# Banded attention in a fused transformer block: the projections of the last two query tiles, and the squares of those tiles, one step later

## The reference

```python
def swa_layer(x, norm_g, w_in, q_g, k_g, sinks, w_out):
    proj = rms_norm_2(x, norm_g) @ w_in
    q, k, v = jnp.split(proj, [C_Q_HEADS * C_HEAD_DIM, C_Q_HEADS * C_HEAD_DIM + kv_w], axis=-1)
    q = rms_norm_2(q.reshape(B, S, C_KV_HEADS, C_GROUP, C_HEAD_DIM), q_g)
    k = rms_norm_2(k.reshape(B, S, C_KV_HEADS, C_HEAD_DIM), k_g)
    ...
# for each block of 128 queries, against its own and the previous block of keys:
        s = jnp.einsum('bqhgd,bkhd->bhgqk', qi.astype(jnp.float32), kb) * scale + bias
        m = jnp.maximum(jnp.max(s, axis=-1, keepdims=True), sink)
        p = jnp.exp(s - m)
        denom = jnp.sum(p, axis=-1, keepdims=True) + jnp.exp(sink - m)
        return jnp.einsum('bhgqk,bkhd->bqhgd', p / denom, vb)
```

## Time and profile before

| | us |
|---|---|
| median of 3 runs | 2206.51 |
| lowest, highest | 2206.43, 2208.19 |
| the profiled execution | 2210.78 |
| its span, first to last instruction | 2209.0 |
| TensorE busy in the span | 2179.2 |
| ScalarE, VectorE, GpSimd busy | 839.3, 899.8, 942.8 |

### The profile page before, as it was taken

The page is one execution under the profiler, slowest core; times in us unless marked ns, Lnnn a source line. Parts: engine busy times, 40 slices in busy tenths (PEclk is TensorE's granted clock), DMA queues, the critical chain, the costliest instruction groups (busy, mean ns, idle before and its releaser), DMA issues.

```text
span 2209.0 us, 28941 instructions
## 1 busy us (share of the span) xinstructions
PE 2179.2 (99%) x10374; PEld 1791.5 (81%) x10374; DVE 899.8 (41%) x1270; ACT 839.3 (38%) x1235; POOL 942.8 (43%) x457
## 2 busy tenths in 40 slices
PE   8999999999999999999999899999999999999999
PEld 6888887788887888888887678888888878888887
DVE  5222222555625522222226854555322556555400
ACT  5222222323533422323334634444323665444421
POOL 3444444333472444445442244444444435444443
PEclk9999999999999999999999999999999999999999
DMA  5333333222352233323341032333333103333332
GB/s 174 100 95 98 101 105 112 77 77 68 105 163 67 75 106 95 95 95 105 105 136 50 29 96 86 96 102 97 105 105 134 49 20 105 95 95 98 101 115 77
DMA packets 58685, 210.25 MB, mean 95 GB/s; under 512 B 6640, under 2 KB 7408, under 8 KB 58224
## 3 DMA queue, kind: packets, MB, share of 16 engines
q1 hardware_dynamic: 56736, 202.07, 29.9%
q10 hardware_dynamic: 1872, 7.10, 0.9%
HBM read 207.05 MB, written 2.10 MB: 95 GB/s over the span
## 4 chain that ended last, share of the span: by engine, by line
PE 95%; DVE 3%; ACT 1%; issue 0%; DMA 0%; ACTq 0%; DVEq 0%
PE psum L217 29%; PE psum L219 29%; PE psum L218 29%; PE psum L241 1%; PE psum L242 1%; PE psum L243 1%; PE psum L1254 1%; PE psum L1279 1%; PE psum L2147 0%; PE psum L2161 0%; ACT swa_p L2244 0%; DVE ab_s L1889 0%; PE psum L2174 0%; DVE ab_negated L1896 0%; PE psum L822 0%
## 5 line engine op out<-in xcount | busy, mean ns | idle before, releaser
L182 POOL TENSOR_TENSOR w_lo<-w_raw,w_hi 128x1024 fp32r<-128x1024 f32 x375 | 902.6, 2414 | 1158.7 <-ACT w_hi L171 1158.6
L217 PE MATMUL psum<-x_hi,w_hi 128*128 128x512 f32 x1816 | 715.1, 394 | 9.6 <-DVE w_lo L189 9.6
L219 PE MATMUL psum<-x_hi,w_lo 128*128 128x512 f32 x1816 | 709.2, 391 | 0.0
L218 PE MATMUL psum<-x_lo,w_hi 128*128 128x512 f32 x1816 | 709.0, 390 | 0.0
L171 ACT ACTIVATE w_hi<-w_raw 128x1024 fp32r<-128x1024 f32 x379 | 394.4, 1054 | 531.3 <-PE psum L219 497.6
L217 PEld LDWEIGHTS psum<-x_hi,w_hi 128*128 128x128 f32 x1816 | 341.9, 188 | 86.6 <-DVE w_lo L189 9.6
L219 PEld LDWEIGHTS psum<-x_hi,w_lo 128*128 128x128 f32 x1816 | 341.5, 188 | 73.1
L218 PEld LDWEIGHTS psum<-x_lo,w_hi 128*128 128x128 f32 x1816 | 341.9, 188 | 71.0 <-issue 0.5
L263 DVE SCALAR_TENSOR_TENSOR x<-psum,x 128x512 f32<-128x512 f32 x64 | 44.3, 692 | 367.4 <-PE psum L219 366.8
L217 PE MATMUL psum<-ffn_hidden_hi,w_hi 128*128 128x512 f32 x352 | 136.9, 389 | 0.0
L218 PE MATMUL psum<-ffn_hidden_lo,w_hi 128*128 128x512 f32 x352 | 136.9, 389 | 0.0
(11 more groups left out here) (311 smaller groups left out, 2515.5 us busy)
## 6 DMA issues: line engine op xcount, KB each, us to landing
w_raw<-in_stream SPq DMA_DIRECT2D x379, 512.0 KB, 3.6
swa_bias<-in_swa_bias ACTq DMA_DIRECT2D x1, 2048.0 KB, 9.8
out<-x SPq DMA_DIRECT2D x8, 256.0 KB, 4.5
ab_bias<-in_ab_bias ACTq DMA_DIRECT2D x1, 1792.0 KB, 7.9
x<-in_x_in SPq DMA_DIRECT2D x4, 256.0 KB, 7.1
x<-in_x_in ACTq DMA_DIRECT2D x4, 256.0 KB, 7.3
xattn_mem<-in_mem ACTq DMA_DIRECT2D x1, 1024.0 KB, 4.9
mix_k_turned<-in_gate_w ACTq DMA_DIRECT2D x1, 256.0 KB, 3.6
```

What stands on the lines that cost most here:

```text
L182: pool.tensor_tensor(self.w_lo[:, split, :], self.w_raw[:, raw, :], self.w_hi[:, split, :].bitcast(F32), ALU.subtract).then_inc(self.w_lo_ ...
L217: pe.matmul(out, w_hi, hi[:, k0 + j, :], start=first and j == order[0], stop=False)
L218: pe.matmul(out, w_hi, lo[:, k0 + j, :], start=False, stop=False)
L219: mm = pe.matmul(out, w_lo, hi[:, k0 + j, :], start=False, stop=last and j == order[-1])
```

## The change

Two tables of numbers change. The projection of q6 moves from step 5 to step 6 and that of q7 from step 7 to step 8; their squares move from steps 6 and 8 to steps 7 and 9. The order of PSUM turns, the copies of weight units (`ahead`) and the `lower` on GpSimd follow from the same tables. No instruction is added or removed.

```diff
-    PROJECTED = {1: [4], 3: [5], 5: [6], 7: [7]}
-    SQUARED = {0: [2, 3], 2: [4], 4: [5], 6: [6], 8: [7]}
+    PROJECTED = {1: [4], 3: [5], 6: [6], 8: [7]}
+    SQUARED = {0: [2, 3], 2: [4], 4: [5], 7: [6], 9: [7]}
```

## The result

| | before | changed |
|---|---|---|
| median, the comparison of 22 runs each, us | 2208.05 | 2211.19 |
| ratio, 95% interval | | 1.0016 (1.0010 to 1.0022) |
| the profiled execution, us | 2210.78 | 2213.35 |
| its span, us | 2209.0 | 2211.5 |
| mean of all runs of this study, us | 2207.05 (171 runs) | 2210.31 (68 runs) |

The change costs 0.16% by the comparison and 3.3 us by the means of all runs (whose scatter is 0.2 and 0.35; the 171 leave out the 22 of the comparison, which have no clock beside them). Forecast were + 1.3 us and no difference beyond 0.2%. The second is right; the size is not, and 2211.19 lies above the range's upper end of 2210.0. Part of that last miss is the base: the range stood on a median of 2206.5 from three runs, and over 22 runs it is 2208.05. Taken as a difference, the range went up to + 3.5 and the medians differ by 3.1.

A forecast was written before the change was run, and what follows sets the result against it. TensorE, busy 2179.2 of 2209.0 us, was taken as the bound, with group 3's root pacing the tail. Root - 0.4 and clock + 1.7 gave + 1.3 us, a forecast median of 2207.8, range 2204.4 to 2210.0.

The forecast's parts named there:

- no difference beyond 0.2%: Whole kernel: the measurement would show no change within 4.4 us; chance 0.88.
- the range's upper end: Total time: 2210.0 us, the forecast plus 0.6 for the stall's upper bound and 1.6 for one more slow stretch.
- The wait of 1.87 ahead of `turn_p(4)`: TensorE behind values(2): with q6 gone from step 5, it waits 1.87 us for copy_turned(3), upper bound 2.5.
- q7 ends 2.94 later, one block less behind it, so the root is 0.4 earlier at full clock: From q7 to group 3's root: + 2.9 us for q7's late end, - 3.3 for less block work behind it.
- The clock falls once, in q6, for 1.7: TensorE in q6's projection: the granted clock falls, costing 1.7 us on the path to q7; bounds 0 and 5.66.
- first rival: In q6's projection: no fall of the clock, so - 0.4 us, 2206.1; chance 0.32.
- the slower rival: From the new wait through q6: clock low throughout, + 5.3 us, 2211.8; chance 0.08, a larger stall included.
- One reason given against a long stretch: In q6: neither earlier fall lasted beyond two 2 us windows, and dense matmuls brought the clock back.
- The tail as before: Behind group 3's root: late waits unchanged, TensorE without a gap after the last, so the root's shift is the total's change.
- The rule of the Trainium skill: At the new wait: clock drops follow idle gaps longer than this one, so the clock would stay up, - 0.4 us.
- The faster rival: TensorE's late waits, step 9 and beyond: up to 4.4 us of them go, 2202.1; chance 0.04.

The follow-up runs named there:

- e1: Against the changed kernel, q7 back in step 7, so only q6's projection and square move; mean 2208.99 us over 22 runs, first ratio to before 1.0009.
- e2: Against the changed kernel, q6 back in step 5, so only q7's projection and square move; mean 2206.58 us, ratio to before 1.0001.
- e11: The changed kernel with the edits of e9 and e10 together; mean 2207.71 us, ratio to before 0.9999.
- e9: The changed kernel with q6's first 9 matmuls between turn_p(4) and the sums of group 2; mean 2209.29 us.
- e10: The changed kernel with 12 matmuls of 256 columns, result unread, in the wait ahead of turn_p(12); mean 2209.22 us.
- e7: e5 with q7's square ahead of block 10's exponentials and lower(7) behind block 13's maxima; mean 2203.72 us, ratios to before 0.9989 and 0.9985.
- e4: The changed kernel with the first 9 of q6's 24 matmuls between values(2) and turn_p(4); mean 2210.07 us.
- e6: The changed kernel with 12 matmuls of 256 columns, result overwritten, in the wait ahead of turn_p(4); mean 2208.40 us.
- after2: The changed kernel again, unedited, for a second profile and more runs; mean 2207.87 us over 12 runs.
- e5: The changed kernel with the column sums of group 2 ahead of turn_p(4) instead of behind it; mean 2206.35 us.

## Why the prediction was wrong

*The wait of 1.87 ahead of `turn_p(4)`*: right, 1.78 to 1.80 in all five profiles. e1 shows it alone: + 1.9 us.

*q7 ends 2.94 later, one block less behind it, so the root is 0.4 earlier at full clock*: right. The third profile, the only one with full clock up to q7's end, has - 0.5, and the take-to-root distance is 8.13 for 8.22 forecast. This compares with a kernel before that had 1.6 us of slow clock ahead of q7. With full clock in both, the changed order is about 1.1 us behind (478.1 against 478.6 - 1.6). Time less loss differs by + 0.3 over all runs; that figure can't confirm the - 0.4, for the limits named above.

*The clock falls once, in q6, for 1.7*: right as a kind and, on the mean, in size, uneven from one execution to the next. After the mark, the waits ahead of `turn_p(12)` end at 65.4, 62.2, 60.6, 62.2 and 62.2 us in the five profiles of the changed kernel, against 61.2 and 61.1 in the two of before: + 4.3, + 1.1, - 0.5, + 1.1, + 1.1. Forecast was + 1.3, its first rival - 0.4, and the first profile is nearest to the slower rival, whose place it has, without its full length. Mean + 1.4. That the mean meets the forecast so well is luck, with single values from - 0.5 to + 4.3. One reason given against a long stretch does not hold: that dense matmuls had brought the clock back. In the kernel before, it was back by 1760, while q7's projection began at 1760.82, and back at about 1780 with no projection near (granted clock 1.00 from 1760 to 1762, 0.98 from 1780 to 1782).

*The tail as before*: this is the step that failed. The prediction took the shift of the root for the change of the total and had TensorE work "without a gap to the end of the stage" behind the last wait, so its forecast has no clock term behind the root at all; only the range's upper end allows for one more slow stretch, without a place. From `turn_p(12)` to `values(15)` the five profiles take 24.8, 24.8, 23.8, 26.5 and 26.5 us; the two of before take 23.8, and so do those of e1 (two) and e2. That is + 1.5 on the mean. Four times in five the clock was at 0.5 for 3.4 or 6.8 us behind the last long wait, under the output projection, where TensorE is the bound again and a slow stretch costs time. The + 1.4 up to `turn_p(12)` and this + 1.5 are the + 2.9 from the mark to the end, beside 3.3 measured over all runs.

The rows show that the missing time is slow clock in the tail: the work there is the same and the waits are no longer. Why it falls there is less sure. e11, which feeds both places, takes 2.6 of the 3.3 back though it adds work, and e9 and e10 took 1.0 and 1.1, each near its scatter. But no run fed the array in some other place, and in the profiles of e9, e10 and e11 the clock fell behind the sums of group 3, 46.5 to 48.5 us after the mark, ahead of the tail's filling.

All twenty profiles together show a pattern. In nine of them (before, e1, e9, e10, e11, e2 and one of five of the changed kernel) the clock fell 46 to 49 us after the mark, behind the sums of group 3 and beside ScalarE's table load and root, and then the tail took 23.8 us. A fall of 3.4 us there is free: from the take of q7 to the root it is 8.13 us and from the root to `turn_p(12)` 13.29, in the third profile of the changed kernel with it as in the first without it. In the nine others, e7's two aside, it did not fall there (in e4 and e6 it fell a little later, at 50), and the tail took 24.2 to 26.5. So the fall seems moved rather than added: from a place where it is free to one where it counts. e7, with shorter waits, has neither.

What decides between the two places stays open. It isn't q7's place close ahead of those sums alone (4.7 us between them instead of 8.2), since e2 has the same 4.7 and its clock fell behind them. It isn't the order alone either, since the changed kernel went both ways. Nor was any run made to vary the moment at which the stage begins, which the expectation of after2 names as a rival.

*The rule of the Trainium skill* (TensorE: Matmul & The Clock Gate, "Why this matters for your kernels"), that drops in the middle of a kernel follow idle gaps longer than this wait: by it the clock would have stayed up. The wait was 1.78 to 1.80 in all five profiles, and the clock fell behind it in four; the measurement decides.

*The faster rival* got nothing in the changed kernel: its waits sum to 5.6 us in the first profile, the new one of 1.8 included, so the late ones are 3.8 for 4.2, with 0.8 more in the middle of the sums.

## What to carry to other kernels

A filler moved by one step must be priced at both ends: where it leaves, look which wait it covered; where small work (column sums, transposes) then stands alone, price a slow stretch of TensorE's clock wherever that engine is the bound next, also far behind the change. A slow stretch that is free where it stands is worth leaving there. The same wait can be filled by work that is already in the program: e5 puts the sums into it, and the combined order (e7) beats both kernels by 3.3 and 6.6 us.

With differences of a tenth of a per cent, put the runs' mean clock beside their time: taking the loss out brought the scatter of one run of before from 2.6 to 1.5 us. It does not say where the clock was lost, or whether that cost anything. For this, count from a mark close ahead of the change in several profiles of the same kernel.

## What the runs showed of the hardware

Executions of one kernel differ by nearly 10 us (2201.7 to 2211.0 for all but one of before's 171 runs), and most of it goes with TensorE's clock (correlation of time and loss 0.93): 32 of 171 runs of before had a mean of 0.997 or more, and 1 had 0.992 or less; of the changed kernel's 68 runs 5 and 14. The same instructions with the same wait ran through the same place at 1.00 in one profile, at 0.5 for 3.4 us in three, and for 10.2 us in one. I had taken one profile's two slow stretches for the kernel's own.
